# Gated block with an S5 scan: modulation work one tile ahead, and one gate unit moved ahead of the chunk inputs

## The reference, cut to what matters

```python
mod   = silu(c)     @ w_ada + b_ada      # sh1, sc1 are needed first
mod_c = silu(c_ctx) @ w_ada + b_ada
h  = rms_norm(x,   g_mix) * (1 + sc1)  + sh1
hc = rms_norm(ctx, g_mix) * (1 + sc1c) + sh1c
u_a, z_b, gate_logits = split(h @ w_in)  # 512, 1024, 2048 columns
u_ac = (hc @ w_in[:, :512])
# S5: discretise A and B, powers of A, scan over the 512 tokens in chunks of 8,
#     both directions, readout with C, gelu, gated linear unit -> y_a
# SGU: gelu(z_b), layer norm, spatial product                  -> y_b
x = x + ga1 * ((g_a * (y_a @ w_pa) + g_b * (y_b @ w_pb)) @ w_out)
x = x + ga2 * conv_ffn(modulate(x))      # depthwise 3x3 convolution, silu gate
out = rms_norm(x, g_final)
```

## Time and profile before

| | |
|---|---|
| median of three runs | 477.63 us |
| profiled execution: time, span | 475.63 us, 473.8 us |
| PE busy in matmuls | 454.2 us, 96% |
| DVE busy | 389.6 us, 82% |
| ACT busy | 104.9 us, 22% |
| u loop on PE (L435, first to last) | 14.9 to 59.4 us |
| gate unit 1 starts | 115.38 us |
| first L599, first L611 | 150.11 us, 159.10 us |
| u gates and projections end, w_out starts | 210.19 us |
| FFN up projection (L714), 704 matmul records | 246.9 to 400 us |

### The profile page before, as it was taken

How to read it: one execution, slowest core, us unless ns; L and a number is a source line. 1 busy time by engine, 2 the same in 40 slices (tenths; PEclk the granted TensorE clock), 3 DMA queues, 4 the chain that set the end, 5 groups by cost and what they waited for, 6 DMA issues and landing times.

```text
span 473.8 us, 7929 instructions
## 1 busy us (share of the span) xinstructions
PE 454.2 (96%) x2736; PEld 359.8 (76%) x2736; DVE 389.6 (82%) x822; ACT 104.9 (22%) x195; POOL 45.8 (10%) x76
## 2 busy tenths in 40 slices
PE   4879999999999999989999999999999999999995
PEld 2657856898888988878878888887888887444454
DVE  4598899999999987961064999998999999899654
ACT  5422255135103144000142211111111011200002
POOL 2001020002203233000000110110110111000000
PEclk9989999999999999999999999999999999999998
DMA  7991599952999999962999433542543443100002
GB/s 292 425 416 48 179 327 126 279 178 65 99 187 416 410 410 410 417 252 89 394 408 395 180 122 145 179 156 109 177 155 116 172 177 120 58 0 0 0 1 89
DMA packets 21932, 96.90 MB, mean 204 GB/s; under 512 B 6480, under 2 KB 7120, under 8 KB 13200
## 3 DMA queue, kind: packets, MB, share of 16 engines
q1 hardware_dynamic: 15024, 74.70, 44.3%
q0 software_dynamic: 5488, 20.19, 13.4%
q10 hardware_dynamic: 1392, 1.63, 1.0%
HBM read 93.91 MB, written 2.59 MB: 204 GB/s over the span
## 4 chain that ended last, share of the span: by engine, by line
PE 80%; DVE 16%; issue 1%; DMA 1%; ACT 1%; DVEq 0%; ACTq 0%
PE bank L714 31%; PE bank L725 14%; PE bank L522 10%; DVE s_region L977 8%; PE bank L679 6%; PE bank L630 6%; PE bank L435 5%; PE bank L611 1%; PE bank L648 1%; PE bank L403 1%; DVE s_region L1233 1%; DMA a_raw<-s5raw 1%; DVE s_region L1096 1%; PE bank L369 1%; DVE merge_tmp L977 1%
## 5 line engine op out<-in xcount | busy, mean ns | idle before, releaser
L714 PE MATMUL bank<-h_all,s_region 128*128 128x256 f32 x704 | 152.4, 380 | 0.7 <-ACT ctx_region L926 0.7
L714 PEld LDWEIGHTS bank<-h_all,s_region 128*128 128x128 f32 x704 | 133.8, 190 | 19.0 <-ACT ctx_region L926 1.1
L1430 DVE SCALAR_TENSOR_TENSOR ctx_region<-ctx_region,pk_sb 128x189 f32<-128x189 f32 (+2 forms) x352 | 127.3, 434 | 0.0
L522 PE MATMUL bank<-h_all,ring_region 128*128 128x256 f32 x256 | 56.2, 381 | 0.3 <-DVE s_region L1264 0.3
L522 PEld LDWEIGHTS bank<-h_all,ring_region 128*128 128x128 f32 x256 | 48.5, 190 | 7.3 <-DVE s_region L1264 0.6
L725 PE MATMUL bank<-s_region,ring_region 128*128 128x512 f32 (+1 forms) x132 | 47.6, 522 | 0.0
L725 PEld LDWEIGHTS bank<-s_region,ring_region 128*128 128x128 f32 x132 | 25.1, 190 | 22.6 <-issue 21.5
L926 ACT ACTIVATE ctx_region<-bank 128x512 f32<-128x512 f32 x22 | 13.1, 597 | 124.8 <-PE bank L714 68.2
L977 DVE TENSOR_TENSOR s_region<-s_region,power 128x2048 f32<-128x2048 f32 (+1 forms) x16 | 38.1, 2419 | 0.1
L435 PE MATMUL bank<-h_all,ring_region 128*128 128x256 f32 x128 | 32.6, 403 | 3.8 <-ACT h_all L794 3.8
L1345 DVE SCALAR_TENSOR_TENSOR s_region<-s_region 128x1024 f32<-128x1024 f32 x28 | 33.6, 1223 | 2.2 <-DMA s_region<-mod_w 1.6
(11 more groups left out here) (211 smaller groups left out, 466.8 us busy)
## 6 DMA issues: line engine op xcount, KB each, us to landing
s_region<-up_w SPq DMA_DIRECT2D x33, 1024.0 KB, 4.8
ring_region<-ring_w SPq DMA_DIRECT2D x26, 1024.0 KB, 8.1
s_region<-mod_w POOLq DMA_DIRECT2D x28, 512.0 KB, 9.9
s_region<-early_w SPq DMA_DIRECT2D x4, 1024.0 KB, 21.6
gates<-early_w SPq DMA_DIRECT2D x2, 1024.0 KB, 10.6
s_region<-k_scratch POOLq DMA_DIRECT2D x8, 256.0 KB, 13.2
x_region<-x_t SPq DMA_DIRECT2D x1, 1024.0 KB, 5.0
ctx_region<-ctx_t SPq DMA_DIRECT2D x1, 1024.0 KB, 7.2
```

The lines of the kernel that those rows point to most:

```text
L522: mx = pe.matmul(bank[5 - j % 2][:, mm * TOK:(mm + 1) * TOK], ring[:, u % RING, (mm * KD + k) * P:(mm * KD + k + 1) * P], h_x[:, k, :], st ...
L714: mx = pe.matmul(bank[s % 3][:, half * TOK:(half + 1) * TOK], up_ring[:, s, (half * KD + k) * P:(half * KD + k + 1) * P], h2[:, k, :], sta ...
L1430: dve.scalar_tensor_tensor(out=o, in0=a, scalar=cw[:, tile[half], (dy + 1) * 3 + dx + 1], in1=o, op0=ALU.mult, op1=ALU.add).then_inc(s_con ...
```

## The change

In the u loop PE's order becomes: rows(0), spread(1), pick(0), the context's squares; then rows(1) ahead of u_of_tile(0, 1). Inside u_of_tile(0, 1), ahead of its third block, come spread(0) and pick(1). Then rows(2), u_of_tile(0, 0), pick(2), and for each later tile: u of x, rows(k + 2), u of the context, pick(k + 2). Before, pick(k + 1) stood between the two halves of tile k; now it is done before tile k begins.

ACT copies row 1 out ahead of its two sines instead of behind modulated(0, 0). DVE's pieces are spread one to a tile: discretise at 1, state_powers at 2, input_matrix at 3, then products and sums, so that w_products(1, 0) moves from tile 7 to behind the loop.

Gate unit 1 moves on PE from behind the SGU product to directly behind gate unit 0, and its two sigmoids on ACT to behind those of unit 0. Jobs 4 and 5 wait for all four sigmoids. Units 2 to 5 keep their place and the wait for DVE's copies of jobs 3 to 5.

```diff
@@ tensor engine, u_of_tile
                     elif k == 0 and v == 1 and m == COLUMN_BANK[0]:
                         pe.wait_ge(s_std, 2)
+                        pe.wait_ge(s_rdiag, 2)
+                        spread(0)
+                        first_pick(1)
@@ tensor engine, the loop
             square_columns(0)
+            first_rows(1)
             u_of_tile(0, 1)
-            pe.wait_ge(s_rdiag, 2)
-            spread(0)
-            first_rows(1)
+            first_rows(2)
             u_of_tile(0, 0)
-            first_pick(1)
-            first_rows(2)
+            first_pick(2)
             for k in range(1, KD):
                 u_of_tile(k, 1)
-                if k + 1 < KD:
-                    first_pick(k + 1)
+                if k + 2 < KD:
+                    first_rows(k + 2)
                 u_of_tile(k, 0)
                 if k + 2 < KD:
-                    first_rows(k + 2)
+                    first_pick(k + 2)
@@ tensor engine, behind z_u
             gate_unit(0)
+            gate_unit(1)
...
-                if job == E_BANKS - 1:
-                    pe.wait_ge(s_gate, 2)
+                if job >= E_BANKS - 2:
+                    pe.wait_ge(s_gate, 4)
...
             pe.wait_ge(s_ev, 3)
-            gate_unit(1)
             for j in range(2, 6):
@@ scalar engine
             token_roots(0)
+            first_rows(1)
             act.wait_ge(s_trig_in, 2)
...
             modulated(0, 0)
-            first_rows(1)
...
             gate_sigmoids(0)
+            gate_sigmoids(1)
...
-            for j in range(1, 5):
+            for j in range(2, 5):
                 gate_sigmoids(j)
@@ vector engine
-            for k in range(KD):
+            normed(0, 1)
+            modulation(0)
+            reciprocal_diagonals(0)
+            normed(0, 0)
+            for k in range(1, KD):
                 normed(k, 1)
-                if k == 0:
-                    modulation(0)
-                    reciprocal_diagonals(0)
                 normed(k, 0)
-                if k == 0:
-                    continue
                 modulation(k)
                 if k == 1:
                     discretise()
+                elif k == 2:
                     state_powers()
-                elif k == 2:
+                elif k == 3:
                     input_matrix()
-                elif k % 2 == 1:
-                    w_products((k - 3) // 4, (k - 3) // 2 % 2)
+                elif k % 2 == 0:
+                    w_products(0, (k - 4) // 2)
                 else:
-                    w_sum((k - 4) // 4, (k - 4) // 2 % 2)
+                    w_sum(0, (k - 5) // 2)
+            w_products(1, 0)
             w_sum(1, 0)
```

## The result

| | before | after |
|---|---|---|
| median, lowest to highest, runs | 477.99 us, 475.95 to 483.25, 20 | 480.37 us, 478.95 to 484.52, 20 |
| profiled execution, span | 475.63 us, 473.8 us | 480.29 us, 478.4 us |
| mean granted clock in it | 0.993 | 0.984 |
| first v matmul (L482, L483) | 59.42 us | 55.91 us |
| scan starts | 116.30 us | 118.07 us |

The ratio is 1.0057, 95% interval 1.0032 to 1.0082: within 2%, but slower by more than the interval, by 0.32 to 0.82%. The profiled executions differ by 4.66 us and the medians by 2.4 us, because that of before, 475.63 us, was quicker than each of its twenty runs here.

A forecast was written before the change was run, and what follows sets the result against it. PE was taken as the bound, with idle time and half clock in the u loop. Terms -3.5, +1.4, +0.9, +1.2, -0.3 gave -0.3 us, the walk -0.6; taken as -0.5 from median 477.63: 477.1 us, range 473.8 to 480.3.

The forecast's parts named there:

- The u loop, -3.5 us: PE up to the v matmuls: 5.2 us of idle time and low clock removed, 1.7 us of early-unit waits added.
- The chunk inputs, -0.3 us: PE's 0.31 us idle time at 115.38 us for DVE's copies of the chunk inputs goes, 0.3 us at most.
- K, +1.4 us: PE reaches L599 at 146.2 us, K is back at 147.6 us, so PE idles 1.4 us.
- The scan's end: Scan starts at 118.5 us behind the SGU product and ends at 157.3 us, when the readout (L611) starts.
- +0.9 for the scan: Ahead of the readout (L611): PE is ready at 156.4 us, the scan ends at 157.3 us, so PE idles 0.9 us.
- The walk: The prediction's step-by-step reckoning by clock times through the kernel, handovers counted; it gave -0.6 us in total.
- DVE's sums without waits, 13.8 us: DVE's 12 sums behind the scan start at 160.5 us and take 12 x 1.15 us, without waits for tiles.
- The gelu's wait of 1.2 us: Ahead of L648: PE is ready at 177.4 us, gelu ends at 178.6 us, so PE idles 1.2 us.
- Rival B: Sums' tiles stay late: 479.4 us; second stage, clock falls behind PE's idle time before L648: 480.3 us. Chance 0.27.
- Rival A: The u loop's gain arrives whole, with no waits for K, scan or sums: 474.1 us, chance 0.15.
- Rival C: The u loop gains nothing, early units land late or DVE's long pieces make PE wait: 481.6 us, chance 0.08.
- three signs of being wrong: Scan starting before 117.5 us, L648 starting later than 179.3 us, or v matmuls starting after 57 us.

The follow-up runs named there:

- e1_loop: The u loop's change alone on the kernel before, gate unit 1 and its sigmoids at their old place: 472.95 us, ratio 0.9907.
- e10_nolead: e1_loop with PE also waiting, ahead of the readout, for DVE's first modulation sum: 477.34 us, ratio 0.9993 to the kernel before.
- e2_gate: The move of gate unit 1 alone on the kernel before, with the old u loop: 485.68 us, ratio 1.0163.
- e9_wait7: The kernel after with the wait for the scan ahead of gate unit 7, the readout behind it: 478.75 us, ratio 1.0028 to before.
- e5_late0: e1_loop with PE also waiting, ahead of the readout, for y_b's last step on DVE: 473.12 us, ratio 0.9898 to before.

## Why the prediction was wrong, step by step

- **The u loop, -3.5 us: right, its last digit by luck.** v started at 55.91 us (predicted 55.9), with no idle time before tile 2 and no half clock. The waits of 1.0 and 0.7 us for the early units are 0.71 and 0.50 us in e1_loop, and hidden in the profile of after by its late clock. With an early clock, as in the profile of before, e1_loop's v started at 55.27 us, 4.15 us earlier than before; the shorter waits are 0.5 us of the difference. DVE's long pieces cost nothing. As a ratio the loop alone is worth 0.6 to 1.3%, 2.8 to 6.1 us, so the sum's -3.5 is inside; by w_out's start in e1_loop (207.46 against 210.19 us) it is 2.7 us, with 0.56 us gone to the wait for y_a.
- **The chunk inputs, -0.3 us: right in kind.** No idle time there any more.
- **K, +1.4 us: wrong.** PE did not wait for it. The store was issued 2.6 us later (predicted 3.0), but K came back at 143.83 us, not 147.6: the gathers took 25.9 us from their first issue instead of 28.5. L600 ran at 145.61 us without a wait. Why the gathers were quicker wasn't tried.
- **The scan's end: right, and the sum of both waits too.** It started at 118.07 us (predicted 118.5) and released the readout at 156.93 us (predicted 157.3). Since PE had not waited for K, the 1.4 + 0.9 = 2.3 us that I had in two pieces came as one of 2.26 us, directly ahead of the readout.
- **The step that failed** is the term "+0.9 for the scan": the wait ahead of the readout was priced at its own length, and the readout and gate unit 7 behind it at their usual duration. The one sentence that says why is "By my likeliest case, with waits of 1.4 us, it stays up", of the clock; that PE could stop again for code was nowhere in the sum. What followed the wait took 6.8 us more (11.85 + 9.03 us instead of 7.10 + 6.95 us), nearly all of it at half clock. The walk had PE ready for L648 at 177.4 us; less the 0.4 us by which the readout was early, and 6.8 us more, is 183.8 us, and L649 started at 183.86 us. This one term explains the whole miss in the profile. That the wait came in one piece of 2.26 us is not the excuse: in e10_nolead, on the kernel with the loop alone, 0.44 us there cost 4.0 us more. What made the clock fall at 159.2 us in after and not as early in e2_gate stays open.
- **DVE's sums without waits, 13.8 us: right** (160.09 to 173.9 us). The gelu's wait of 1.2 us did not come, as PE was later still; DVE waited for PE instead.
- **Rival B** had the sign and nearly the size (479.4 and 480.3 us), by another road: its first stage, sums' tiles that stay late, did not happen, and its second put a fallen clock behind an idle time of near 3 us before L648. The row that it leaned on the earlier trace rows was the right one, applied to the wrong wait; its number is near by luck. The Trainium skill, "TensorE: Matmul & The Clock Gate", section Loop structure matters more than you think, was cited there: a long wait between matmuls makes PE go cold, that is, drop to its lower clock. The kernel after agrees (clock 0.50 behind 2.26 us, 11.85 us for a stage of 7.10), and e9_wait7 shows a wait of the same length behind which the clock stayed at 1.00. **Rival A** needed the second half away: e1_loop is what A described, 0.9% faster. **Rival C** is out.

Of the three signs of being wrong that I named, two did not come (the scan started behind 117.5 us, v ahead of 57 us); the third, L648 later than 179.3 us, came.

## What to carry to other kernels

A wait that a sum prices at its own length can have a second price in what comes behind it. Look at what stands directly behind: here a stage of many short instructions was clean when its signal came 0.9 us before PE, and cost 4.0 us more when it came 0.44 us after. When work is moved ahead of a hand-over chain, test the halves by themselves; here one was worth 0.9% and the other cost 1.6%, and the pair looked like little.

## What the runs showed of the hardware that I had not expected

- 0.44 us of standing at a wait led to a stop of 1.96 us, 4.4 us later; with 0.9 us of lead it did not come. The stop ends 2.4 us behind the start of a 16 KB instruction packet; all fourteen gaps marked "issue" in the twelve profiles end 2.2 to 2.6 us behind one.
- The length of an idle time did not tell whether the clock falls. Behind 2.26 and 2.75 us ahead of the narrow 64x32 matmuls it fell 2.3 and 2.1 us into the readout, though PE was busy for 99% of that stretch in the kernel after, and stayed at half for 13.7 us. Behind 2.26 us ahead of the same matmuls in e2_gate it held for 4.3 us of work, and behind 2.27 us ahead of 128x128 ones in e9_wait7 to the end of the readout. In e5_late0 it fell at 16.4 us, for 3.4 us, behind a wait of only 1.03 us for early unit 1.
- PE's clock at the start of an execution comes up at different times: at 9.9 us in before and 10.3 us in e1_loop, at 15.9 us in after and 15.7 us in e2_gate. L380's pair took 1.22 us at 14.21 us in the kernel after and 0.70 us at 12.92 us in e1_loop. In after this hid the waits for the early units, so a difference of 1 to 2 us between two profiles can lie in their first 16 us.
